# Eight experts finished before the next one's products, the last tile's shift on TensorE and its rows stored in halves, and one weight load moved

## The chip, the core and the metric

The kernel runs on one core of a Trainium2 chip, in one launch. The metric is the device time of that launch in microseconds (us), the median of several runs. The engines are named as in the profile: PE is TensorE (PEld its weight loads), DVE VectorE, ACT ScalarE, POOL GpSimd, SP SyncE. SyncE only issues DMAs here; ScalarE and GpSimd issue some too.

## What is computed

One layer of a diffusion trunk, on 128 context tokens and 512 latent tokens of width 1024. A modulation from a condition vector, a mixing sub-layer (windowed attention beside a gated MLP over chunks, then an output projection) and a channel sub-layer, a mixture of 32 experts, of which each token takes two:

```
h2 = rms_norm(x, g_pre_ffn) * (1 + scale2) + shift2
g_prob = softmax(h2 @ router_group); g_top, g_idx = top_k(g_prob, 1)
e_top, e_idx = top_k(expert logits of that group, 2)
weights = softmax(e_top) * g_top
hid = silu(h2 @ w_gate[e]) * (h2 @ w_up[e])          # per chosen expert
f = sum over the two experts of weight * (hid @ w_down[e])
x = x + gate2 * rms_norm(f, g_post_ffn)
```

Each expert has w_gate, w_up (1024 x 256) and w_down (256 x 1024) in float32: 1 MB each, 3 MB for an expert, 96 MB in all.

## The kernel before, in words

The 640 tokens are five tiles of 128 (TILES = 5; the last is number 4, `KEPT`). The program is written out engine by engine, with semaphores between them; there is no scheduler, and each engine runs its instructions in the order in which its block writes them.

In the tail of the mixing sub-layer, for each tile, TensorE does the output projection (L762), VectorE the residual, and three things follow from it. TensorE turns the residual (`turn_res`) and makes the router's logits (`router`), from which VectorE makes the choice of experts (`route`, L1311 to L1334) and each token's rank in its expert (`rank`); TensorE helps with `prefix` and `pick`. GpSimd multiplies the residual by the scale (L1787), ScalarE by the token's norm (`scaled`, L1652), GpSimd adds the shift (L1793, `st_bc[:, 1]`): this is h2, and a DMA stores it as rows in DRAM (`h2_dram`, in the profile `h_rows`). For tiles 0 to 3 SyncE issues the store, for the last one ScalarE (L1657). `keep_warm` issues matmuls whose result nobody reads.

When all rows are stored and the row indices are made (`rows_made`, L1373), GpSimd gathers for each expert the rows of its tokens by indirect DMAs (`gather`, L1800), up to 64 tokens in one tile; experts with more tokens have a second tile (`xg_x`, inside the `If` of each engine's `expert`). An expert is: turn the gathered rows (`next_x`), the gate and up products (`products`, L909), silu on ScalarE (L1682) and the multiplication on VectorE (L1440), turn the result (L532), the down product (L917), a copy, and a scatter of the result rows by GpSimd (L1809).

Two orders of this exist. With `late` false, expert e+1's gate and up products stand on TensorE ahead of expert e's down product. With `late` true, expert e's down product and its second tile come first, then `expert_done` is raised, and then follow expert e+1's products. `late = e < EARLY or e >= LATE`, with EARLY = 3 and LATE = 26.

The weights have seven slots (WS = 7), four in `ring`, the others in space that attention or the residual used (`w_5`, `w_5d`, `w_6`, `w_6d`, `w_7`; in the profile `w`, `w_5d`, `w_6d`). SyncE issues the loads in one queue. Expert e's load (from 7 on) waits for the down product and `expert_done` of expert e-7 and for the landing of expert e-2's (L454 and L455). The loads of experts 0 to 6 stand before that, between the stores of rows; the w_down of expert 4 (`load_down(4)`) is issued when the last tile's `mixg` is there.

Of the kernel before, what the change touches and what calls it, by code (L numbers as in the profile page):

```python
# [14 lines left out]
P = 128  # L15
# [3 lines left out]
TILES = (CTX + LAT) // P  # L19
# [27 lines left out]
XS = 3  # L47
LS = 4
LATE = EXPERTS - 6
EARLY = 3  # L50
KEPT = TILES - 1
ADDED = 3
GATE_SLOT = 25
# [58 lines left out]
def hybrid_dit_step(  # L112
# [4 lines left out]
    with ExitStack() as ctx:  # L117
# [74 lines left out]
        rows = sb("rows", [N_ROWS, P], F32, b0 + 2 * KB)  # L192
        gm_u = sb("gm_u", [P, TILES, GM], F32, b0)
        h2 = sb("h2", [P, 2, D], F32, b0)
# [20 lines left out]
        st_bc = sb("st_bc", [P, 2, D], F32, t0 + 4 * KB)  # L215
# [50 lines left out]
        def const(name):  # L266
            a, b = CONST_COLS[name]
            return cst[:, a:b] if b <= N_KEPT else cst_once[:, a - N_KEPT:b - N_KEPT]

        ident = const("ident")  # L270

        ps = ctx.enter_context(nc.psum_tensor("ps", [P, 8, 512], F32))
# [3 lines left out]
        h2_dram = nc.dram_tensor("h2_rows", [TILES * P, D], F32, kind="Internal").ap()  # L276
# [31 lines left out]
        op0_mm, op_mm, sq2, ms2, rs2, mixg, res1, sq3, ms3, rs3 = (  # L308
            sem(n) for n in ("op0_mm", "op_mm", "sq2", "ms2", "rs2", "mixg", "res1", "sq3", "ms3", "rs3"))
        t2_tr, t2_dve, t2_act, h2_mul, h2_sc, h2_done = (  # L310
            sem(n) for n in ("t2_tr", "t2_dve", "t2_act", "h2_mul", "h2_sc", "h2_done"))
        h2_out = [sem("h2_out0"), sem("h2_out1")]
        st_in, w_made, sh_mm = (sem(n) for n in ("scale_shift_in", "router_made", "shift_mm"))
# [65 lines left out]
        def _(sp):  # L379
# [64 lines left out]
            def load_down(e):  # L444
                sp.dma_start(weights(e)[1], w_down[0, e].rearrange("(k p) f -> p k f", p=P)).then_inc(wd_in[e % LS], 16)
# [44 lines left out]
            load_half(5, 1)  # L490
            sp.wait_ge(op_mm, TILES)
            load_expert(RING - 1)
            sp.wait_ge(mixg, 2 * TILES)
            load_down(4)
            sp.wait_ge(rt_mm, TILES)
            sp.wait_ge(sq3, 2 * TILES)
            sp.wait_ge(h2_out[0], 16 * 3)
            sp.wait_ge(h2_out[1], 16 * 2)
            for j in range(XS):
                sp.wait_ge(xg_in[j], 16)  # L500
            sp.wait_ge(rows_made, ALL_ROWS)
            sp.wait_ge(w_made, W_TOK)
            sp.wait_ge(e_in, 16)
# [26 lines left out]
        def _(pe):  # L530
# [99 lines left out]
            for i in range(TILES):  # L630
                if i >= 2:
                    pe.wait_ge(kv_read, i - 1)
                for k in range(KC):
                    last = pe.matmul(ps[:, i % 2, 0:2 * KVW], h_t[:, k, i * P:(i + 1) * P], w_kv[:, k, :],
                                     start=(k == 0), stop=(k == KC - 1))
# [56 lines left out]
            for i in range(TILES):  # L692
# [3 lines left out]
                for cc in range(4):  # L696
                    last = transpose(ps[:, 4 + i % 4, cc * P:(cc + 1) * P], gm_u[:, i, cc * P:(cc + 1) * P])
# [140 lines left out]
            def prefix(i):  # L838

                pe.wait_ge(r_both, i + 1)  # L840
                if i:
                    pe.wait_ge(r_rank, i)
                for m in range(i + 1):
                    last = pe.matmul(ps[:, 7, 64:64 + EXPERTS], before_b[:, :] if m == i else ones_b[:, :], both[:, m, :],
                                     start=(m == 0), stop=(m == i))
                last.then_inc(r_pos, 1)
# [24 lines left out]
            def keep_warm(n):  # L871

                for _ in range(n):
                    pe.matmul(ps[:, 2, :], ident, mix_t[:, KEPT, 0:4, :].rearrange("p k q -> p (k q)"), start=True, stop=True)

            prefix(TILES - 2)
            pe.wait_ge(mixg, 2 * (TILES - 1))
            pe.wait_ge(sq2, 2 * (TILES - 1))
            keep_warm(3)
            turn_res(TILES - 1)  # L880
            router(TILES - 1)
            pick(TILES - 2)
            keep_warm(3)
            prefix(TILES - 1)
            pick(TILES - 1)
            pe.wait_ge(r_rank, TILES)
            for m in range(TILES):
                last = pe.matmul(ps[:, 7, 96:96 + EXPERTS], ones_b[:, :], both[:, m, :], start=(m == 0), stop=(m == TILES - 1))
            last.then_inc(r_idx, 1)
            keep_warm(2)  # L890

            def pick_extras():
# [43 lines left out]
            def expert(e):  # L936
                c = e
                wgu, wd = weights(e)
                late = e < EARLY or e >= LATE
                xb = e % 2 if late else (e + 1) % 2  # L940
# [42 lines left out]
        def _(dve):  # L983
# [458 lines left out]
            def expert(e):  # L1442
                c = e
                late = e < EARLY or e >= LATE
                xb = e % 2 if late else (e + 1) % 2
# [52 lines left out]
        def _(act):  # L1498
# [41 lines left out]
            for z, ks in enumerate(((1,), (3,), (6, 7))):  # L1540
                act.wait_ge(s_pre, z + 1)
                for k in ks:
                    for cn, (a, b) in enumerate(((0, P), (P, TILES * P))):
                        last = act.activation(h_t[:, k, a:b], h_t[:, k, a:b], ACT.Identity,
                                              bias=pre[:, 0, 1, k, cn:cn + 1], scale=pre[:, 0, 0, k, cn:cn + 1])
# [21 lines left out]
            for u in range(2 * TILES):  # L1567
                i = u % TILES
# [78 lines left out]
            def scaled(i):  # L1647
                act.wait_ge(rs3, i + 1)
                for hh in range(2):
                    act.wait_ge(h2_mul, 2 * i + hh + 1)  # L1650
                    part_ = h2[:, i % 2, 512 * hh:512 * (hh + 1)]
                    act.activation(part_, part_, ACT.Copy, scale=stats[:, 7, i:i + 1]).then_inc(h2_sc, 1)  # L1652
                if i < KEPT:
                    act.dma_start(out_rows(i), res[:, i]).then_inc(res_out, 16)
                else:
                    act.wait_ge(h2_done, 2 * TILES)
                    act.dma_start(h2_dram[i * P:(i + 1) * P, :], h2[:, i % 2]).then_inc(h2_out[i % 2], 16)  # L1657

            act.wait_ge(w_made, 1)
            for i in range(TILES):  # L1660
# [23 lines left out]
            def expert(e):  # L1684
                c = e
                late = e < EARLY or e >= LATE
                if not late:
# [42 lines left out]
        def _(pool):  # L1730
# [31 lines left out]
            for t in range(TILES * PAIRS):  # L1762
                i = t // PAIRS
                w = P * (1 if i == 0 else 3 if i in (1, 4) else 4)
                pool.wait_ge(inv_made, t + 1)
                for a in range(KVH):
                    p = probs[:, t % 4, a, 0:w]
                    last = pool.tensor_scalar(p, p, att_stats[:, INV, t, a:a + 1], 1.0, ALU.mult, ALU.mult)  # L1768
# [8 lines left out]
            for i in range(TILES):  # L1777
                pool.wait_ge(ms2, i + 1)
                rsqrt(stats[:, 4, i:i + 1], stats[:, 3, i:i + 1], 1, rs2)
                if i < 2:  # L1780
                    pool.wait_ge(st_in, 16 * (i + 1))
                else:
                    pool.wait_ge(h2_out[i % 2], 16 * (i // 2))
                for hh in range(2):
                    pool.wait_ge(res1, 2 * i + hh + 1)
                    cut_ = slice(512 * hh, 512 * (hh + 1))
                    pool.tensor_tensor(h2[:, i % 2, cut_], res[:, i, cut_], st_bc[:, 0, cut_], ALU.mult).then_inc(h2_mul, 1)  # L1787
                pool.wait_ge(ms3, i + 1)
                rsqrt(stats[:, 7, i:i + 1], stats[:, 6, i:i + 1], 1, rs3)
                for hh in range(2):  # L1790
                    pool.wait_ge(h2_sc, 2 * i + hh + 1)
                    cut_ = slice(512 * hh, 512 * (hh + 1))
                    pool.tensor_tensor(h2[:, i % 2, cut_], h2[:, i % 2, cut_], st_bc[:, 1, cut_], ALU.add).then_inc(h2_done, 1)  # L1793
# [38 lines left out]
                                            y_x[:, :], None, bounds_check=2 * TOPK * TILES * P - 1,  # L1832
                                            oob_is_err=False).then_inc(e_st, 16)

            pool.wait_ge(h2_out[0], 16 * 3)
            pool.wait_ge(h2_out[1], 16 * 2)
            pool.wait_ge(rows_made, FIRST_ROWS)
            for c in range(XS):
# [15 lines left out]
            for e in range(EXPERTS):  # L1854
                late = e < EARLY or e >= LATE
                if not late:
# [46 lines left out]
```

## Time and profile before

| what | before |
|---|---|
| median of 3 runs | 634.27 us (633.21 to 635.83) |
| the profiled execution | 633.7 us, its span 631.8 us |
| TensorE busy | 541.1 us, 86% of the span |
| VectorE, ScalarE, GpSimd busy | 183.5, 149.5, 178.1 us |
| read and written in DRAM | 163.75 and 16.68 MB, 286 GB/s over the span |
| expert stage, from the first gather | 333.9 us to the end |
| the chain that ended last, by engine | TensorE 66%, DMA 23%, VectorE 4%, the rest 7% |
| granted TensorE clock, mean | 0.956 |

Busy time is the time in which an engine had an instruction running; a high share does not say that the engine bounds the kernel. Which wait ends last in a stage is read from the chain and from the waits. A clock of 1.00 in the windows is 2.4 GHz, 0.50 is 1.2 GHz. A DMA share of 1.00 in a window means that all 16 DMA engines worked all the time.

### The profile page before, as it was taken

The numbers are of one execution on the slowest core, as the hardware profiler recorded it, in microseconds if no ns is written. First come the engines' busy times: TensorE is split into PE (matmuls) and PEld (weight loads), VectorE is DVE, ScalarE is ACT, GpSimd is POOL, SyncE is SP. The second block draws the span as 40 slices with busy tenths as digits, with TensorE's granted clock in tenths as the row PEclk, the third lists the DMA queues.
The fourth block names the chain that finished last, engine by engine and source line by source line (L and its number), as shares of the span: only waits on it lengthen the run. The fifth ranks groups of instructions, "written<-read, shape, count | busy, mean of one in ns | idle before, by whom it ended". The sixth has DMA issues, their size and how long they took to land.

```text
span 631.8 us, 10117 instructions
## 1 busy us (share of the span) xinstructions
PE 541.1 (86%) x3527; PEld 309.2 (49%) x3527; DVE 183.5 (29%) x581; ACT 149.5 (24%) x374; POOL 178.1 (28%) x247
## 2 busy tenths in 40 slices
PE   2899999999889999999977799899998888878700
PEld 2654764444666664555534455565655444434300
DVE  2210340002368861444485111111111101111026
ACT  4401021012047761222230111111111111111133
POOL 1000300014404440344445233243433123321214
PEclk9999999999998999999996999999999888999965
DMA  9999742060799304421692999799999999999178
GB/s 321 369 380 387 225 171 98 16 251 0 206 303 408 154 1 170 170 93 68 240 383 72 399 409 396 275 409 405 406 401 399 381 397 402 398 410 408 70 311 203
DMA packets 59075, 173.21 MB, mean 274 GB/s; under 512 B 5804, under 2 KB 11492, under 8 KB 58112
## 3 DMA queue, kind: packets, MB, share of 16 engines
q1 hardware_dynamic: 50608, 153.76, 64.5%
q0 software_dynamic: 7216, 15.77, 8.0%
q10 hardware_dynamic: 1184, 2.81, 1.2%
q8 instruction: 40, 0.66, 0.4%
q14 instruction: 27, 0.22, 0.1%
HBM read 163.75 MB, written 16.68 MB: 286 GB/s over the span
## 4 chain that ended last, share of the span: by engine, by line
PE 66%; DMA 23%; DVE 4%; issue 2%; ACT 2%; SPq 1%; POOL 1%; ACTq 0%; POOLq 0%; DVEq 0%
PE ps L909 12%; PE ps L762 11%; PE ps L652 11%; PE ps L532 8%; DMA ring<-in_w_down_dram 8%; PE ps L917 6%; PE ps L606 6%; DMA ring<-in_w_up_dram 4%; PE ps L549 4%; DMA w<-in_w_down_dram 3%; PE ps L714 3%; DMA w_6d<-in_w_down_dram 3%; PE ps L739 2%; DMA out_dram<-v_all 1%; DMA cst_once<-in_consts_dram 1%
## 5 line engine op out<-in xcount | busy, mean ns | idle before, releaser
L909 PE MATMUL ps<-ring,xt 128*64 128x256 f32 x704 | 84.9, 396 | 14.9 <-DMA ring<-in_w_up_dram 10.6
L909 PEld LDWEIGHTS ps<-ring,xt 128*64 128x64 f32 x704 | 55.3, 142 | 51.0 <-DMA ring<-in_w_up_dram 16.8
L652 PE MATMUL ps<-ring,h_t 128*128 128x512 f32 x160 | 69.5, 593 | 0.0
L1440 DVE TENSOR_TENSOR hid<-act_g,ps 128x128 f32<-128x128 f32 x32 | 9.2, 288 | 198.0 <-ACT act_g L1682 198.0
L909 PE MATMUL ps<-w,xt 128*64 128x256 f32 x416 | 49.4, 391 | 8.1 <-DMA w<-in_w_up_dram 5.2
L762 PE MATMUL ps<-ring,mix_t 128*128 128x512 f32 x120 | 53.6, 596 | 0.0
L1809 POOL DMA_INDIRECT expert_results<-y_sb,idx_out x32 | 32.5, 1015 | 63.6 <-ACT y_sb L1696 62.2
L652 PEld LDWEIGHTS ps<-ring,h_t 128*128 128x128 f32 x160 | 30.1, 190 | 36.8 <-issue 36.8
L909 PEld LDWEIGHTS ps<-w,xt 128*64 128x64 f32 x416 | 33.5, 140 | 27.8 <-DMA w<-in_w_up_dram 8.8
L1800 POOL DMA_INDIRECT xg<-h_rows,idx_in x32 | 34.6, 1081 | 28.2 <-POOL idx_in L1798 22.5
L917 PE MATMUL ps<-ring,hid_t 128*64 128x512 f32 x160 | 38.7, 605 | 2.5 <-ACT hid_t L1692 2.5
L1682 ACT ACTIVATE act_g<-ps 128x128 f32<-128x128 f32 x32 | 8.9, 277 | 133.5 <-PE ps L909 133.5
L606 PE MATMUL ps<-ring,h_t 128*128 128x512 f32 x80 | 35.6, 597 | 1.9 <-issue 1.9
L762 PEld LDWEIGHTS ps<-ring,mix_t 128*128 128x128 f32 x120 | 22.2, 190 | 25.8 <-issue 25.7
L1768 POOL TENSOR_SCALAR probs<-probs,att_stats 128x384 f32<-128x384 f32 (+2 forms) x40 | 22.9, 586 | 42.1 <-DVE att_stats L1220 42.1
L1733 POOL TENSOR_TENSOR stats<-stats,half_pow 128x1 f32<-128x1 f32 x20 | 15.4, 772 | 67.7 <-DVE stats L1264 40.5
L1696 ACT COPY y_sb<-ps 128x512 f32<-128x512 f32 x32 | 18.7, 585 | 66.5 <-PE ps L917 66.5
L1733 POOL TENSOR_TENSOR gm_stats<-gm_stats,half_pow 128x8 f32<-128x8 f32 x5 | 9.7, 1942 | 80.4 <-DVE gm_stats L1161 80.4
L549 PE MATMUL ps<-ring,cond 128*32 128x128 f32 x768 | 24.5, 281 | 1.6 <-issue 1.5
L1798 POOL COPY idx_in<-src_row 128x1 uint32<-128x1 uint32 x29 | 5.3, 184 | 71.6 <-PE ps L532 71.6
L549 PEld LDWEIGHTS ps<-ring,cond 128*32 128x32 f32 x768 | 21.4, 113 | 6.5 <-issue 6.1
L606 PEld LDWEIGHTS ps<-ring,h_t 128*128 128x128 f32 x80 | 14.7, 190 | 19.5 <-issue 19.5
(243 smaller groups left out, 732.1 us busy)
## 6 DMA issues: line engine op xcount, KB each, us to landing
ring<-in_w_mod_dram SPq DMA_DIRECT2D x10, 2048.0 KB, 12.4
ring<-in_w_gate_dram SPq DMA_DIRECT2D x20, 1024.0 KB, 9.4
ring<-in_w_up_dram SPq DMA_DIRECT2D x20, 1024.0 KB, 14.4
ring<-in_w_down_dram SPq DMA_DIRECT2D x20, 1024.0 KB, 16.5
w<-in_w_gate_dram SPq DMA_DIRECT2D x12, 1024.0 KB, 8.0
w<-in_w_up_dram SPq DMA_DIRECT2D x12, 1024.0 KB, 13.5
y_back<-expert_results SPq DMA_DIRECT2D x5, 1024.0 KB, 8.8
ring<-in_w_mod_dram SPq DMA_DIRECT2D x4, 1024.0 KB, 12.8
```

What stands on the lines that cost most here:

```text
L532: return pe.matmul(out, in_, ident[0:n_in, 0:n_in], is_transpose=True, start=True, stop=True)
L549: last = pe.matmul(ps[32 * g:32 * g + 32, b % 2, 0:P], cond[:, k, :], w[:, k, g * P:(g + 1) * P], start=(k == 0), stop=(k == KC - 1))
L606: last = pe.matmul(ps[:, 3 + i, 0:ATT], h_t[:, k, i * P:(i + 1) * P], w_q[:, k, :], start=(k == 0), stop=(k == KC - 1))
L652: last = pe.matmul(ps[:, 4 + u % 4, :], h_t[:, k, i * P:(i + 1) * P], w[:, k, :], start=(k == 0), stop=(k == KC - 1))
L714: last = pe.matmul(ps[:, 2 * (t % 2) + a, pos * P:(pos + cnt) * P], q_t[half, g, i * P:(i + 1) * P], k_t[half, first * P:(first + cnt) * P ...
L762: last = pe.matmul(ps[:, 2 * (i % 2) + hh, :], mix_t[:, i, k, :], rhs, start=(k == 0), stop=(k == KC - 1))
L909: last = pe.matmul(bank[fh * SLOT:(fh + 1) * SLOT, 0:FE].rearrange("p (a f) -> p a f", a=2), x_t[:, k % 4, (k // 4) * SLOT:(k // 4 + 1) * ...
L917: last = pe.matmul(bank[ch * SLOT:(ch + 1) * SLOT, :], h[:, fh * SLOT:(fh + 1) * SLOT], w[:, fh, ch * 512:(ch + 1) * 512], start=(fh == 0) ...
L1733: pool.tensor_tensor(dst, src, half_pow[:, 0:n], ALU.pow).then_inc(done, 1)
L1768: last = pool.tensor_scalar(p, p, att_stats[:, INV, t, a:a + 1], 1.0, ALU.mult, ALU.mult)
L1800: pool.indirect_dma_start(xg[:, j, :], None, h2_halves, bass.IndirectOffsetOnAxis(ap=idx_in[:, j, 0:1], axis=0), bounds_check=2 * TILES * ...
L1809: pool.indirect_dma_start(y_halves, bass.IndirectOffsetOnAxis(ap=idx_out[:, c, 0:1], axis=0), y_buf(e), None, bounds_check=2 * TOPK * TILE ...
```

## The change

`EARLY` goes from 3 to 8, so experts 3 to 7 change to the `late` order on all engines. For the last tile, TensorE adds the shift: it first writes the shift into two PSUM banks by an identity matmul, then accumulates the scaled h2 on top, half by half; ScalarE copies each half back into `h2` and issues its store. GpSimd leaves out its addition for that tile. Two groups of three `keep_warm` matmuls go, and the last group of two waits for ScalarE's copies, as it writes the same bank. In SyncE's queue `load_down(4)` moves behind the waits for the stored rows and for the first three gathers. The counts on `h2_out[0]` rise by one store.

```diff
-EARLY = 3
+EARLY = 8
@@ SyncE
-            sp.wait_ge(mixg, 2 * TILES)
-            load_down(4)
             sp.wait_ge(rt_mm, TILES)
             sp.wait_ge(sq3, 2 * TILES)
-            sp.wait_ge(h2_out[0], 16 * 3)
+            sp.wait_ge(h2_out[0], 16 * 4)
             sp.wait_ge(h2_out[1], 16 * 2)
             for j in range(XS):
                 sp.wait_ge(xg_in[j], 16)
+            sp.wait_ge(mixg, 2 * TILES)
+            load_down(4)
@@ TensorE
+            def last_shift(rows):
+                for hh in range(2):
+                    cut_ = slice(512 * hh, 512 * (hh + 1))
+                    if rows:
+                        pe.wait_ge(h2_sc, 2 * KEPT + hh + 1)
+                    last = pe.matmul(ps[:, 2 + hh, :], ident, h2[:, KEPT % 2, cut_] if rows else st_bc[:, 1, cut_],
+                                     start=not rows, stop=rows)
+                    if rows:
+                        last.then_inc(sh_mm, 1)
...
-            keep_warm(3)
+            pe.wait_ge(st_in, 16 * 2)
+            last_shift(False)
             turn_res(TILES - 1)
             router(TILES - 1)
             pick(TILES - 2)
-            keep_warm(3)
+            last_shift(True)
...
+            pe.wait_ge(h2_done, 2 * TILES)
             keep_warm(2)
@@ ScalarE
-                    act.wait_ge(h2_done, 2 * TILES)
-                    act.dma_start(h2_dram[i * P:(i + 1) * P, :], h2[:, i % 2]).then_inc(h2_out[i % 2], 16)
+                    for hh in range(2):
+                        half = slice(512 * hh, 512 * (hh + 1))
+                        act.wait_ge(sh_mm, 3 + hh)
+                        act.copy(h2[:, i % 2, half], ps[:, 2 + hh, :]).then_inc(h2_done, 1)
+                        act.wait_ge(h2_done, 2 * i + hh + 1)
+                        act.dma_start(h2_dram[i * P:(i + 1) * P, half], h2[:, i % 2, half]).then_inc(h2_out[i % 2], 16)
@@ GpSimd
-                for hh in range(2):
+                for hh in range(2 if i < KEPT else 0):
                     pool.wait_ge(h2_sc, 2 * i + hh + 1)
...
-            pool.wait_ge(h2_out[0], 16 * 3)
+            pool.wait_ge(h2_out[0], 16 * 4)
```

How the instructions stand on TensorE around the last tile, as a difference (`res` is the residual, `h_92` is h2, `cst` the identity):

```order
 L844 MATMUL ps<-both,before_b 128x32
-L874 MATMUL ps<-mix_t,cst 128x512 x3
+L881 MATMUL ps<-st_bc,cst 128x512 x2
 L532 MATMUL ps<-cst,res 128x128 x8
 L834 MATMUL ps<-w_rs,res_t 128x36 x8
 L852 MATMUL ps<-code_oh,sel_slot 128x64 x2
-L874 MATMUL ps<-mix_t,cst 128x512 x3
+L881 MATMUL ps<-h_92,cst 128x512 x2
 L844 MATMUL ps<-both,ones_b 128x32 x4
 L844 MATMUL ps<-both,before_b 128x32
```

Both groups of three are gone; in their places stand the shift (from `st_bc`) and the scaled rows.

TensorE from expert 3's products on, before (`w_129` holds expert 4's gate and up weights, `hid` is expert 3's):

```order
L909 MATMUL ps<-ring,xt 64x256 x16
L532 MATMUL ps<-cst,xg 128x128 x4
L909 MATMUL ps<-w_129,xt 64x256 x16
L532 MATMUL ps<-cst,hid 128x128
L532 MATMUL ps<-cst,xg 128x128 x4
L917 MATMUL ps<-ring,hid_t 64x512 x4
```

The same place after the change (lines after `last_shift` are 12 higher, so L909 is L921 and L917 is L929):

```order
L921 MATMUL ps<-ring,xt 64x256 x16
L532 MATMUL ps<-cst,xg 128x128 x4
L532 MATMUL ps<-cst,hid 128x128
L929 MATMUL ps<-ring,hid_t 64x512 x4
...
L966 UNCONDITIONAL_BRANCH
L921 MATMUL ps<-w_129,xt 64x256 x16
L532 MATMUL ps<-cst,xg 128x128 x4
```

Expert 4's products have moved behind expert 3's down product and the branch around its second tile.

SyncE's queue around `load_down(4)` (`w_5d`), as a difference, with the semaphores that each waits for:

```order
 L440 DMA ring<-in_w_up_dram 128x2x1024
 L445 DMA ring<-in_w_down_dram 128x2x1024
-L445 DMA w_5d<-in_w_down_dram 128x2x1024 [waits mixg]
-L445 DMA w_6d<-in_w_down_dram 128x2x1024 [waits xg_in1,xg_in2,xg_in0,rows_made,h2_out1,router_made,h2_out0,extra_in,sq3,rt_mm]
+L445 DMA w_5d<-in_w_down_dram 128x2x1024 [waits xg_in0,xg_in1,h2_out1,xg_in2,h2_out0,mixg,sq3,rt_mm]
+L445 DMA w_6d<-in_w_down_dram 128x2x1024 [waits extra_in,router_made,rows_made]
 L440 DMA w_133<-in_w_gate_dram 128x2x1024
```

The waits for the stored rows and the gathers now stand ahead of the load of `w_5d` and no longer behind it.

## Rows read from the trace of the kernel before

**Rows 1.** Pieces of the chain that ended last in order of time: start us, us, what
```profile
474.26 17.14 DMA w<-in_w_down_dram
...
575.51 3.67 PE ps L909 x32
```

**Rows 2.** Waits of SyncE's DMA queue, 300 to 600 us: total us, times, longest us
```profile
SPq L455 <- PEq L965: 48.2, 7, 14.0
SPq L454 <- DMA ring<-in_w_up_dram: 47.3, 13, 4.9
...
SPq L503 <- DMA xg_x<-h_rows,idx_x: 3.4, 1, 3.4
```

**Rows 3.** Timeline, SyncE's queue: start us, us, engine line op out<-in
```profile
345.96 0.37 SPq L445 DMA_DIRECT2D w_6d<-in_w_down_dram  x1
...
364.62 0.37 SPq L440 DMA_DIRECT2D ring<-in_w_gate_dram  x1
...
371.53 0.37 SPq L440 DMA_DIRECT2D ring<-in_w_gate_dram  x1
...
383.07 0.37 SPq L440 DMA_DIRECT2D ring<-in_w_gate_dram  x1
...
398.82 0.37 SPq L440 DMA_DIRECT2D w<-in_w_gate_dram  x1
...
405.28 0.37 SPq L440 DMA_DIRECT2D w<-in_w_gate_dram  x1
...
411.45 0.37 SPq L440 DMA_DIRECT2D w<-in_w_gate_dram  x1
...
419.30 0.37 SPq L440 DMA_DIRECT2D ring<-in_w_gate_dram  x1
```

**Rows 4.** Windows: from:to us, length, busy us of five engines, PEclk, DMA share, GB/s
```profile
332.00:346.00 14.00, 11.09 (x64) 6.38 (x66) 8.39 (x35) 0.54 (x2) 8.93 (x11) 0.67 0.24 67
347.00:395.00 48.00, 41.83 (x301) 24.53 (x297) 6.80 (x14) 6.75 (x18) 15.72 (x25) 1.00 1.01 398
394.00:401.00 7.00, 4.71 (x33) 2.31 (x31) 0.29 (x1) 1.13 (x3) 1.32 (x3) 1.00 0.34 95
401.00:575.00 174.00, 155.92 (x1073) 87.19 (x1069) 23.50 (x48) 27.26 (x74) 56.45 (x93) 0.97 1.02 401
```

**Rows 5.** The chain again: expert 4's second tile is turned
```profile
389.27 0.69 PE ps L532 x4
```

**Rows 6.** Timeline, tile 3 and the last tile: start us, us, engine line op
```profile
299.74 0.23 DVE L1319 TENSOR_SCALAR r_e<-r 128x4 f32<-128x4 f32 x1
...
322.58 0.58 ACT L1645 COPY res_t<-ps 128x512 f32<-128x512 f32 x1
...
325.15 2.82 PE L874 MATMUL ps<-mix_t,cst 128*128 128x512 f32 x6
...
325.52 1.33 ACT L1652 ACTIVATE h<-h,stats 128x512 f32<-128x512 f32 x2 [1.74 <-POOL stats L1733]
...
326.32 2.48 POOL L1793 TENSOR_TENSOR h<-h,st_bc 128x512 f32<-128x512 f32 x2 [0.83 <-ACT h L1652]
...
326.67 0.94 DVE L1319 TENSOR_SCALAR r_e<-r 128x4 f32<-128x4 f32 x1
...
327.53 1.30 DVE L1320 TENSOR_SCALAR r_e<-cst,r_s 128x4 f32<-128x4 f32 x1
...
332.43 0.22 DVE L1373 TENSOR_SCALAR idx_in<-ps,cst 128x3 uint32<-128x3 f32 x1 [0.38 <-PE ps L852]
...
333.89 1.17 POOL L1800 DMA_INDIRECT xg<-h_rows,idx_in  x1 [5.08 <-DMA h_rows<-h]
```

**Rows 7.** The chain again: the store of the last tile's rows
```profile
328.83 4.19 DMA h_rows<-h
```

**Rows 8.** DMAs that touch h_rows, 240 to 345 us
```profile
DMA to landing us min/median/max: 2.6/2.9/5.6
```

**Rows 9.** Windows, the microsecond in which the granted clock falls
```profile
331.00:332.00 1.00, 0.08 (x4) 0.00 (x0) 0.85 (x4) 0.62 (x1) 0.00 (x0) 0.53 0.96 393
```

## The prediction

> **What bounds the kernel now.** I read the page's chain first. Its shares (in the table above) name TensorE for two thirds and DMA for a quarter, which is an average over stages. So I read the chain in order of time next. It runs through TensorE until 474 us; from there to 575.5 it holds only weight loads and their issues, the first of them 17.14 us from issue to landing [rows 1]; then come the last two experts on TensorE and the end. The weight stream alone sets the time at which the last expert can be computed. A faster TensorE in the stream's own stretch is worth nothing; what counts is when the stream gets started and whether it ever stands still.
>
> The waits of SyncE's queue say when it does. It waited for TensorE's "expert done" seven times, 48.2 us in total, and after that for landings [rows 2]. Those seven are the loads of experts 7 to 13, since expert e's load takes the slot of expert e-7. Issued were expert 5's w_down at 345.96, expert 8 at 364.62, 9 at 371.53, 10 at 383.07, 11 at 398.82, 12 at 405.28, 13 at 411.45 and 14 at 419.30 [rows 3]. I then looked at what the 16 DMA engines did at these times. From 347 to 395 they were full, share 1.01. Before, from 332 to 346, they had a share of 0.24. And from 394 to 401 there is a hole: seven microseconds at a share of 0.34, so 7 x 0.66 = 4.6 us in which the DMA engines had nothing, because expert 11's load was not issued before 398.82. From 401 to 575 the share is 1.02 [rows 4]. So there are two holes, one of 4.6 us behind expert 4 and one ahead of 347, and the change touches both.
>
> **Eight experts in the late order.** Experts 3 to 7 now do transpose, down product, second tile and "done" before the next expert's gate and up products. This adds no instruction. In the late order an expert without a second tile takes 371.53 - 364.62 = 6.91 us from slot to slot [rows 3]. Expert 2 is done at 371.53 as before. Expert 3 then is done at 378.44 instead of 383.07. Expert 4 would be done at 385.35 without its second tile, which ran from 389.27 [rows 5] to the issue at 398.82 and costs 9.55; it ends at 394.90. Expert 11's load is issued 3.9 us earlier from this part alone. The loads of 12 and 13 follow at 6.91 each, which is less than the roughly 10 us that the full stream took for an expert at that point ((419.30 - 398.82)/2, as expert 14 waits for expert 12's landing), so no new hole opens.
>
> The late order also costs TensorE something, since the handoffs through ScalarE and VectorE are bare: 6.91 us against the 411.45 - 405.28 = 6.17 of an expert in the other order [rows 3], so some 0.7 for each of five experts, 3.7 us in all. The stream hides it: it needs some 10 us for an expert, so TensorE has slack from expert 8 on. Without that cover it is a loss, which is a rival below. GpSimd's gather three experts ahead now stands behind the scatter and the second tile; it still has more than two experts, over 13 us, so I price it at nothing.
>
> **The last tile's shift on TensorE.** GpSimd's two additions, 2.48 us from 326.32, go [rows 6]. In their place come two 512-wide matmuls that lay down the shift early, beside the wait for the residual (nothing), two with h2, and two copies on ScalarE. A kept-warm matmul of the same shape took 2.82/3 = 0.94, a 512-wide copy from PSUM 0.58 [rows 6]. The scaled halves are ready at about 326.2 and 326.85 (325.52 + 1.33). The matmuls end at about 327.2 and 328.1, the second copy at 328.7, and the second half is issued at about 328.8. Before, the whole store was issued at 328.83 [rows 7]. So the addition itself is worth nothing on that path; only the first half leaves 0.9 earlier.
>
> What it does give is on VectorE. Two tiny operations of the last route took 0.94 and 1.30 while GpSimd was adding, and ended with its two halves; the same line took 0.23 for tile 3 with GpSimd quiet [rows 6]. Without the additions 2.24 - 0.46 = 1.8 us leave the path to the row indices: they stand at 332.65 - 1.8 = 330.85 instead of 332.65. This is bounded below by nothing, if something else holds VectorE, and above by the 1.8.
>
> **Store in halves and the moved load.** The store of the last tile took 4.19 us [rows 7] with the DMA engines full; the usual one of these rows took 2.9 [rows 8]. The change takes 1 MB (expert 4's w_down) out of that queue: 1.05 MB at 400 GB/s is 2.6 us. It halves what the last store carries. For the second half I have no row: 1.45 us if it were proportional to bytes, 4.19 if nothing helps. I take 2.5, near the quiet store of 2.9. It lands at 331.3, after the indices; the gathers began 0.87 after the landing before (333.02 to 333.89) [rows 6, 7], so now at about 332.2, that is 1.7 us earlier. The ends are 2.2 (indices decide, 330.85 + 0.87) and 0.
>
> The Trainium skill (DMA: Bandwidth & Descriptors, section Anatomy of one DMA) speaks against halves: each DMA pays a fixed part of about 2.0 us whatever its size, mostly the confirmation of the last byte. By it, the half would take an estimated 2.0 + 0.26 MB at 436 GB/s = 2.6 us and the gathers would start 1.6 earlier, not 2.2. The trace agrees so far that its 512 KB stores never took less than 2.6 [rows 8].
>
> Everything on TensorE from the gathers to expert 4 follows them, so it moves by these 1.7. The moved load is issued when the three first gathers have landed. SyncE waited for the extra gather 3.4 us up to 345.96 [rows 2, 3], so they had landed by 342.5, now by 340.8; the load fills the hole ahead of 347 and is needed only at expert 4. Queued behind it are the wait for the extra gather and the loads of 5 and 6. That gather now shares the engines with 1 MB, which may cost it between 0 and 2.6 us. I take 0.9, so the stream begins 0.8 earlier rather than 1.7.
>
> **Sum.** Expert 11's load is issued 3.9 + 1.7 = 5.6 us earlier. The stream in front of it ends 0.8 earlier, so there are 4.6 + 0.8 = 5.4 us of hole that can be closed, and the hole closes wholly. The gain is the smaller, 5.4 us, and the stream hands it on to the end, since it is full from 401 to the last load and what follows is unchanged. The profiled execution took 633.7 (span 631.8 and 1.9 around it) and would take 628.3. It lay 0.6 below the median of 634.27; against the median I predict 628.9.
>
> **Rivals.** (1) The gathers don't start earlier: the half store lands late, or the matmuls are slow. Speaking for it: the clock. The granted clock fell to 0.53, near the lower of its two levels (1.2 against 2.4 GHz), after TensorE had stood still from 328.0 [rows 6, 9]; the change takes out warming matmuls and has TensorE wait twice for other engines in this tile. At half clock the two h2 matmuls take 1.9 each, the store leaves about 1.9 later and eats the 1.7. Against it: it still did its work at full clock after shorter stops. The gain is then 3.9, 630.4. The Trainium skill (TensorE: Matmul & The Clock Gate, Part 1) has the slow clock as the default that recent activity lifts; by it this rival is open, and no run here shows yet where TensorE's fall would now come.
>
> (2) The hole stays for the larger part, as the weights' order or the gather of the extra rows, not TensorE's slot, sets expert 11's issue. Speaking for it: the extra gather of the second tile is issued by GpSimd, whose order changed. Against it: it is in flight since the tile before. Half of 3.9 remains, 632.3.
>
> (3) Slower: the end is set by TensorE, not by the stream. Its place is experts 3 to 13, its price the five bare handoffs, 3.7 us, less the 1.7 from the gathers: 2.0 slower, 636.3; with rival 1 it is 3.7 slower, 638.0. It decides if TensorE still waits for no weights after 474. The chain's TensorE pieces up to 474 speak for it, SyncE's landing waits from expert 14 on and the full DMA share against it.
>
> **How the numbers follow.** Forecast 0.62, rival 1 0.20, rival 2 0.12, rival 3 0.06. A change of 0.5%, 3.2 us, is about what can be told from none, so faster means below 631.1. Nearly all of the forecast and three quarters of rival 1 lie there, 0.77; within are what is left of both and rival 2 but for a hundredth, 0.16; slower are rival 3 and that hundredth, 0.07. The likeliest case alone spans 628.2 (the gathers 2.2 earlier and the hole no limit: 3.9 + 2.2 = 6.1) to 629.6 (the gathers 0.8 earlier: 4.7). The range takes in rival 1 whole and rival 2 up to its value and leaves 1.2 us below the likeliest case, about the 1.1 by which the lowest of the three runs lies under their median: 627.0 to 632.3.
>
> **What would show it.** Right: expert 11's load issued near 393, DMA share near 1 from 346 to the last load, the issues from expert 14 on about 5.4 earlier; the two tiny VectorE operations at 0.23; the gathers near 332.2; expert 4's w_down near 341. Wrong: a hole in the DMA share elsewhere between 346 and 401; a granted clock of 0.5 before 328; the last store landing after 332; or TensorE instead of loads in the chain behind 474.

## The result and the profile after

| | before | changed |
|---|---|---|
| median of 20 runs | 634.22 us | 631.38 us |
| ratio, 95% interval | | 0.9949 (0.9933 to 0.9965) |
| profiled execution, its span | 633.7, 631.8 us | 628.56, 626.7 us |

One of the 20 runs of each kernel took over 1900 us; the medians count it, while the ratios, here and below, leave out runs over 1.5% above the fastest of their kernel (also 683.11 us in move_only, and 636.17 in warm3_all_late, with which its ratio would be some 0.001 higher). By the ratio the change gives 3.2 us, 2.1 to 4.3; the medians differ by 2.8. The two profiled executions differ by 5.1, but 1.76 of that was there before the first changed instruction. The load of expert 3, which no edit touches, was issued at 318.84 before and at 317.08 after. From here on I count times in the last tile and behind it from that issue, and call it L3. The last row of results is made by VectorE at L3 + 307.17 before (626.01) and at L3 + 303.59 after (620.67), a gain of 3.6 within the changed stretch. (A second trace of the changed kernel, in the table below, has 1.7.)

SyncE's queue after the change; the first row is L3, the others are the loads of expert 5's w_down and of experts 8 to 12, 14 and 15 (start us, us, engine line):

```profile
317.08 0.37 SPq L440 DMA_DIRECT2D ring<-in_w_gate_dram  x1
...
344.70 0.37 SPq L445 DMA_DIRECT2D w_6d<-in_w_down_dram  x1
...
362.72 0.37 SPq L440 DMA_DIRECT2D ring<-in_w_gate_dram  x1
...
369.77 0.37 SPq L440 DMA_DIRECT2D ring<-in_w_gate_dram  x1
...
377.81 0.37 SPq L440 DMA_DIRECT2D ring<-in_w_gate_dram  x1
...
393.47 0.37 SPq L440 DMA_DIRECT2D w<-in_w_gate_dram  x1
...
400.64 0.37 SPq L440 DMA_DIRECT2D w<-in_w_gate_dram  x1
...
414.63 0.37 SPq L440 DMA_DIRECT2D ring<-in_w_gate_dram  x1
...
426.19 0.37 SPq L440 DMA_DIRECT2D ring<-in_w_gate_dram  x1
```

Against [rows 3]: expert 8's load is at L3 + 45.64 (before 45.78) and expert 9's at 52.69 (52.69), so nothing came early before the reordered experts. Expert 11's is at L3 + 76.39 (79.98), 3.6 earlier. Expert 5's w_down is at L3 + 27.62 (27.12), half a microsecond later. The windows, to be laid beside [rows 4] (from:to us, busy us of five engines, granted clock, DMA share, GB/s):

```profile
319.00:321.00 2.00, 0.87 (x6) 0.63 (x7) 1.73 (x3) 0.90 (x3) 0.79 (x1) 1.00 1.01 408
321.00:323.00 2.00, 1.89 (x15) 1.69 (x13) 1.52 (x2) 1.02 (x3) 2.00 (x2) 0.82 1.04 426
323.00:329.00 6.00, 5.45 (x18) 2.92 (x18) 3.77 (x24) 2.51 (x4) 0.64 (x2) 0.50 0.70 278
392.00:399.00 7.00, 5.39 (x41) 3.54 (x41) 0.98 (x2) 1.13 (x3) 1.39 (x4) 1.00 0.80 290
399.00:573.00 174.00, 159.75 (x1116) 91.17 (x1114) 23.48 (x48) 27.37 (x73) 58.73 (x96) 0.98 1.02 402
```

The hole behind expert 4 has gone from 4.6 to 7 x 0.20 = 1.4 us, and behind it the stream is full, as before. The other thing to see is the clock in the first three rows. It falls to 0.50 (1.2 GHz) in the last tile; before, it stayed at 1.00 there until 331. Two rows of the kernel before, the router's matmuls and the window ahead of its fall [rows 9]:

```profile
323.31 1.95 PE L834 MATMUL ps<-w_rs,res_t 128*128 128x36 f32 x16
...
330.00:331.00 1.00, 0.21 (x5) 0.19 (x5) 0.90 (x6) 0.98 (x3) 0.00 (x0) 1.00 1.06 422
```

The last tile after the change in the timeline, against [rows 6]:

```profile
321.55 2.92 PE L834 MATMUL ps<-w_rs,res_t 128*128 128x36 f32 x16
...
324.54 3.78 PE L881 MATMUL ps<-h,cst 128*128 128x512 f32 x4
...
325.59 0.23 DVE L1331 TENSOR_SCALAR r_e<-r 128x4 f32<-128x4 f32 x1
325.73 0.22 DVE L1332 TENSOR_SCALAR r_e<-cst,r_s 128x4 f32<-128x4 f32 x1
...
328.36 0.59 ACT L1671 COPY h<-ps 128x512 f32<-128x512 f32 x1 [1.12 <-PE ps L881]
...
328.97 0.33 ACTq L1673 DMA_DIRECT2D h_rows<-h  x1
...
329.75 0.22 DVE L1385 TENSOR_SCALAR idx_in<-ps,cst 128x3 uint32<-128x3 f32 x1 [0.33 <-PE ps L852]
...
331.88 1.48 POOL L1816 DMA_INDIRECT xg<-h_rows,idx_in  x1 [8.15 <-DMA h_rows<-h]
```

VectorE's two small operations are at 0.23 and 0.22, as forecast. The two h2 matmuls took 3.78 instead of the 1.88 forecast. The second half left at L3 + 11.89, 1.9 later than the whole store before (9.99). The chain says what its landing took (answers to [rows 7]):

```profile
328.97 2.04 DMA h_rows<-h
```

That is 2.04 instead of 4.19. So it landed 0.2 us earlier than before, and the gathers started at L3 + 14.80 against 15.05.

### The profile page after: what moved, and what is told of

Same layout as the page of the kernel before. It is cut to its first block, busy times and chain, and to the rows that moved or that the text cites. A ratio compares the mean times of both kernels' runs of the same rounds, so it can differ in the third digit from the quotient of the medians.

```text
span 626.7 us, 10110 instructions
## 1 busy us (share of the span) xinstructions
PE 538.8 (86%) x3523; PEld 308.4 (49%) x3523; DVE 181.7 (29%) x581; ACT 150.8 (24%) x376; POOL 175.2 (28%) x245
## 4 chain that ended last, share of the span: by engine, by line
PE 60%; DMA 29%; DVE 3%; issue 2%; SPq 2%; ACT 2%; POOL 1%; ACTq 0%; POOLq 0%; DVEq 0%
PE ps L762 11%; PE ps L652 11%; DMA ring<-in_w_down_dram 11%; PE ps L921 8%; PE ps L532 7%; PE ps L606 6%; PE ps L929 4%; DMA ring<-in_w_up_dram 4%; PE ps L549 4%; DMA w_5d<-in_w_down_dram 4%; PE ps L714 3%; DMA w<-in_w_down_dram 3%; DMA w_6d<-in_w_down_dram 3%; PE ps L739 2%; DMA ring<-in_w_mod_dram 2%
## 5 line engine op out<-in xcount | busy, mean ns | idle before, releaser
L921 PE MATMUL ps<-ring,xt 128*64 128x256 f32 x704 | 83.1, 389 | 12.4 <-DMA ring<-in_w_up_dram 7.1
L921 PEld LDWEIGHTS ps<-ring,xt 128*64 128x64 f32 x704 | 55.4, 140 | 46.1 <-issue 13.6
L921 PE MATMUL ps<-w,xt 128*64 128x256 f32 x416 | 49.4, 391 | 5.0 <-DMA w<-in_w_up_dram 2.7
L921 PEld LDWEIGHTS ps<-w,xt 128*64 128x64 f32 x416 | 33.8, 140 | 25.1 <-issue 10.4
L929 PE MATMUL ps<-ring,hid_t 128*64 128x512 f32 x160 | 38.7, 605 | 3.3 <-ACT hid_t L1708 2.8
L532 PE MATMUL ps<-cst,xg 128*128 128x128 f32 x128 | 22.5, 302 | 4.3 <-DMA xg<-h_rows,idx_in 4.3
L1613 ACT ACTIVATE probs<-probs,att_stats 128x384 f32<-128x384 f32 (+2 forms) x40 | 24.0, 600 | 0.0
```

The costliest lines, as they stand in the source:

```text
L532: return pe.matmul(out, in_, ident[0:n_in, 0:n_in], is_transpose=True, start=True, stop=True)
L921: last = pe.matmul(bank[fh * SLOT:(fh + 1) * SLOT, 0:FE].rearrange("p (a f) -> p a f", a=2), x_t[:, k % 4, (k // 4) * SLOT:(k // 4 + 1) * ...
L929: last = pe.matmul(bank[ch * SLOT:(ch + 1) * SLOT, :], h[:, fh * SLOT:(fh + 1) * SLOT], w[:, fh, ch * 512:(ch + 1) * 512], start=(fh == 0) ...
L1613: last = act.activation(probs[:, t % 4, a, 0:width(t)], probs[:, t % 4, a, 0:width(t)], ACT.Exp, bias=att_stats[:, NM, t, a:a + 1], scale= ...
```

## The experiments

All ratios are to the kernel before, run on the same chip at the same time (the interval is of 95%). Since the edits are worth 1 or 2 us, the better instrument is the trace, counted from L3. The table gives TensorE's clock in the h2 matmuls, the issue of the (second half) store, the first gather, the load of expert 5's w_down, expert 11's load, and the last result row.

| kernel | ratio | clock | store | gather | w_down 5 | load 11 | last row |
|---|---|---|---|---|---|---|---|
| before | 1 | - | 9.99 | 15.05 | 27.12 | 79.98 | 307.17 |
| changed | 0.9949 | 0.5 | 11.89 | 14.80 | 27.62 | 76.39 | 303.59 |
| changed, again | 0.9942 (0.9923-0.9961) | 0.5 | 11.77 | 14.67 | 29.77 | 77.41 | 305.49 |
| early_only | 0.9966 (0.9940-0.9992) | - | 10.00 | 15.03 | 26.97 | 77.25 | 305.42 |
| tail_only | 1.0001 (0.9977-1.0026) | 0.5 | 11.89 | 14.78 | 27.90 | 79.79 | 306.70 |
| move_only | 0.9971 (0.9952-0.9989) | - | 9.99 | 14.78 | 27.45 | 79.99 | 307.42 |
| early5 | 0.9995 (0.9974-1.0016) | 0.5 | 11.89 | 14.80 | 27.04 | 76.35 | 306.83 |
| warm | 0.9935 (0.9909-0.9961) | 1.0, then 0.5 | 11.46 | 14.37 | 27.01 | 75.85 | 304.01 |
| warm2 | 0.9916 (0.9883-0.9948) | 1.0 | 10.23 | 13.13 | 26.48 | 74.74 | 303.03 |
| warm3 | 0.9927 (0.9900-0.9955) | 1.0 | 10.23 | 13.12 | 27.22 | 74.58 | 302.41 |
| warm3, again | 0.9929 (0.9904-0.9954) | 1.0 | 10.22 | 13.13 | 26.77 | 75.86 | 303.86 |
| warm3_nomove | 0.9928 (0.9904-0.9951) | 1.0 | 10.23 | 15.06 | 26.91 | 76.41 | 304.32 |
| warm3_all_late | 0.9919 (0.9886-0.9952) | 1.0 | 10.23 | 13.13 | 27.36 | 76.43 | 304.56 |
| extra_first | 0.9915 (0.9889-0.9940) | 1.0 | 10.23 | 13.13 | 26.03 | 73.44 | 301.37 |

The two kernels that were profiled twice show what one trace is worth. Up to the first gather they agree within 0.15 us; expert 11's load moves by 1.0 and 1.3 and the last row by 1.9 and 1.5, among other things because expert 0's products run at the lower clock for a varying part (they took 4.25 us in the changed kernel's first trace and 5.43 in its second) and because the gather of the second tile landed 3.3 us after its issue in the one and 5.6 in the other. In two rows the second trace missed what was expected of it below: the clock fell at L3 + 7.4, not within 6, and expert 11's load came at 77.41, not at 76.2 to 76.5.

**One part at a time.** The late order alone (early_only), the rest alone (tail_only), the moved load alone (move_only):

```diff
-EARLY = 3        # early_only: the kernel before with
+EARLY = 8
-EARLY = 8        # tail_only: the changed kernel with
+EARLY = 3
```

> The kernel before with EARLY = 8 and nothing else. Theory A (the late order of experts 3 and 4 is all that the change gained; the rest came to nothing because TensorE's clock fell in the last tile): expert 11's load comes about 3.7 us earlier after the load of expert 3 than before (76.3 instead of 80.0 us), the hole in the DMA share behind expert 4 shrinks from 4.6 to about 1 us, and the time is about 3.5 us below before, like the whole change. Rival B (the moved load and the last tile gave part of it): less than 2.5 us below before.

> The changed kernel with EARLY back at 3: the last tile's shift on TensorE, the halved store and the moved load alone. Theory A: the granted clock falls to half in the router's matmuls of the last tile, the gathers start as long after the load of expert 3 as before (14.8 to 15.1 us), and the time is that of before within 1 us. Rival B: 1.5 us or more below before.

The last tile's edits and the moved load without the late order give nothing, as theory A said, and the hole stays. The late order alone gives 2.2 us by the ratio (0.5 to 3.8), short of the 3.5 expected and inside what rival B allowed, though the interval takes in both and the medians differ by 3.1. Its expert 11's load came 2.7 earlier and not 3.7; in this trace expert 0's products took 5.30 us instead of 4.37, at the lower clock for the first three and a half. The hole behind expert 4 shrinks to 7 x 0.20 = 1.4 us, as in the changed kernel. The windows of tail_only and of early_only:

```profile
392.30:399.30 7.00, 4.70 (x33) 2.30 (x31) 0.29 (x1) 1.13 (x3) 1.33 (x3) 1.00 0.41 140
390.00:397.00 7.00, 5.77 (x42) 3.35 (x43) 0.00 (x0) 0.81 (x2) 1.20 (x2) 1.00 0.80 283
```

I can't tell its 2.2 from the whole change's 3.2: the intervals overlap.

> The kernel before with only the load of expert 4's w_down moved. Theory A: the last tile's store takes about 3 us instead of 4.2, the gathers start about 0.4 us earlier at most, since the row indices then decide (332.65 in the kernel before), the hole behind expert 4 stays, and the time is that of before within 0.5 us. Rival B: over 1 us faster.

```diff
             sp.wait_ge(op_mm, TILES)
             load_expert(RING - 1)
-            sp.wait_ge(mixg, 2 * TILES)
-            load_down(4)
...
                 sp.wait_ge(xg_in[j], 16)
+            sp.wait_ge(mixg, 2 * TILES)
+            load_down(4)
```

The whole store took 2.6 us instead of 4.2, with the load out of its way. Gathers 0.3 earlier and then nothing, as expected: the indices, ready at L3 + 13.81 in the kernel before, now decide. Expert 11's load is where it was before, and the last row within 0.3. The ratio nonetheless says 1.8 us faster (0.7 to 3.0). No row of the trace has that, and I leave it open; it is a warning against reading the ratios of the other kernels to the microsecond.

**Only experts 3 and 4 in the late order.**

```diff
-EARLY = 8
+EARLY = 5
```

> The changed kernel with EARLY = 5, so only experts 3 and 4 change their order. Theory A (the hole is behind expert 4, so only these two matter): the time of the changed kernel within 0.7 us. Rival E (the loads of experts 12 to 14 also have to come early): a new hole in the DMA share after expert 11's load, and 1 us or more slower than the changed kernel.

Theory A fell, rival E was right. Windows of early5, in which L3 is 318.15:

```profile
393.00:400.00 7.00, 4.93 (x40) 3.40 (x40) 0.98 (x2) 0.86 (x2) 1.38 (x3) 1.00 0.77 262
400.00:404.00 4.00, 4.00 (x37) 3.01 (x34) 0.16 (x1) 0.47 (x2) 1.05 (x1) 1.00 1.02 415
404.00:408.00 4.00, 4.00 (x29) 2.15 (x30) 0.82 (x2) 0.64 (x2) 1.80 (x4) 1.00 0.36 96
```

Expert 11's load comes as early as with EARLY = 8, but the DMA engines stand again 4 x 0.64 = 2.6 us in the third row. The loads of experts 11 and 12 show why:

```profile
394.50 0.37 SPq L440 DMA_DIRECT2D w<-in_w_gate_dram  x1
406.14 0.37 SPq L440 DMA_DIRECT2D w<-in_w_gate_dram  x1
```

They lie 11.6 apart. Expert 4, the last late one, is followed by the products of 5, and expert 5, back in the other order, has those of 6 ahead of its own down product. So the products of two experts lie between two releases of a slot. With EARLY = 8 that pause lies between the loads of experts 14 and 15 (414.63 to 426.19 above, also 11.6), where the loads of experts 13 and 14 are still under way and the DMA engines stay full (share 1.02 or 1.03 from 414 to 430). The late order has to reach as far as the stream has no reserve, not only to the expert with the hole.

**The clock.** Is the missing gain the clock? First one warmer ahead of the shift matmuls, as many microseconds of work as the three warmers before:

```diff
+            keep_warm(1)
             last_shift(False)
```

> The changed kernel with one warming matmul (0.94 us) ahead of the two that lay down the shift, so that TensorE has the same 2.8 us of work there as before. Theory A: the granted clock stays at 1.0 until the h2 matmuls are done, these take 1.9 us instead of 3.8, the second half store leaves 1.5 to 1.9 us earlier relative to the load of expert 3, the gathers start 1.5 us or more earlier, and the time is 1.5 us below the changed kernel, some 5 us below before. Rival C (the clock falls anyway, as TensorE stands before the h2 matmuls): half clock at the h2 matmuls as in the changed kernel, and its time. Rival D (the clock stays, but the gathers' landings, not their start, hold the experts): gathers earlier, no time gained.

Rival C, mostly. Windows of warm (L3 is 317.50):

```profile
321.50:323.50 2.00, 1.90 (x18) 1.69 (x17) 1.60 (x2) 0.95 (x3) 2.00 (x2) 1.00 1.03 422
323.50:325.50 2.00, 1.01 (x7) 0.65 (x7) 1.13 (x9) 1.31 (x2) 0.56 (x2) 0.98 1.03 422
325.50:327.50 2.00, 2.00 (x4) 0.65 (x2) 1.73 (x12) 0.61 (x2) 0.00 (x0) 0.50 0.67 262
```

The clock holds through the router's matmuls, but TensorE then stands about 1 of 2 us waiting for ScalarE (second row), and beside the h2 matmuls the clock is at 0.50 (third row; they take 3.35). In the four traces of kernels with the changed kernel's tile it fell between L3 + 5.1 and 7.4, here at 7.9. So that stop was filled too, with a matmul into bank 4, whose turned residual has been copied out by then, and a third one stands behind the h2 matmuls (`keep_warm` takes the bank as a second argument here):

```diff
             pick(TILES - 2)
+            keep_warm(1, 4)
             last_shift(True)
+            keep_warm(1, 4)
             prefix(TILES - 1)
```

> The changed kernel with three warming matmuls: one ahead of the shift, one between the pick of tile 3 and the h2 matmuls, one behind them (the last two into a PSUM bank that is free by then). With one warmer the granted clock fell 7.9 us after the load of expert 3, while TensorE stood 1 us before the h2 matmuls. Theory A: with that stop filled the clock stays at 1.0 there, the second half store is issued at about 10.0 us after the load of expert 3 instead of 11.9, the gathers start at about 13.0 instead of 14.8, and expert 11's load comes some 1.7 us earlier than in the changed kernel; the time is 1.5 us below it. Rival C: the clock falls all the same and nothing is gained over the kernel with one warmer. Rival F: the store leaves earlier but the row indices or the descriptors hold the gathers at 14 or later.

Windows of warm2 (L3 is 316.93), the same three stretches as shown for the changed kernel, and its timeline:

```profile
319.00:321.00 2.00, 1.72 (x9) 0.79 (x8) 1.58 (x3) 1.05 (x3) 0.94 (x1) 1.00 0.99 383
321.00:323.00 2.00, 1.90 (x18) 1.69 (x16) 1.62 (x2) 0.87 (x3) 1.93 (x2) 1.00 1.02 420
323.00:329.00 6.00, 4.92 (x27) 2.23 (x26) 4.42 (x26) 3.96 (x7) 0.55 (x1) 1.00 0.83 326
```

```profile
324.39 1.98 PE L881 MATMUL ps<-h,cst 128*128 128x512 f32 x4
...
327.16 0.33 ACTq L1676 DMA_DIRECT2D h_rows<-h  x1
...
328.68 0.22 DVE L1388 TENSOR_SCALAR idx_in<-ps,cst 128x3 uint32<-128x3 f32 x1 [0.33 <-PE ps L852]
...
330.06 1.17 POOL L1819 DMA_INDIRECT xg<-h_rows,idx_in  x1 [6.48 <-DVE dst_row L1388]
```

The clock stays at 1.00, the matmuls take 1.98, the store leaves 1.7 earlier than in the changed kernel, and the gathers start at L3 + 13.13, 1.9 before the old 15.05. Expert 11's load is 5.2 earlier than before. Theory A held in every row that it named. The ratio is 5.3 us below before (3.3 to 7.4).

With more warmers at the end, until the first rows land:

```diff
-            keep_warm(2)
+            keep_warm(5)
```

> The same with five warming matmuls instead of two behind the last pick, so that TensorE works until the first gathered rows land. Theory A: the turning of the first rows and expert 0's products run at full clock, 1.3 instead of 1.95 us and 3.7 instead of 4.3, so expert 11's load comes up to 1.2 us earlier than in the kernel with three warmers. Rival: the clock was full again by then anyway, or falls in the wait of the gathers whatever is done, and the time is the same within 0.3 us.

The first rows are turned in 1.41 (1.92 in warm2) and expert 0's products take 3.67 (4.65), so the clock is held there as well. But TensorE then only waits for the gathered rows of expert 0's second tile, which became the late one. Expert 11's load gains 0.2, not 1.2 (and in the second trace of warm3 it comes 1.1 later than warm2's).

> warm3 once more, on the same chip as the changed kernel: if the clock is what the change lost, 1.0 to 1.8 us below the changed kernel; if the forecast's term for the gathers is simply not there, the same within 0.5 us.

> The changed kernel once more, for comparison on one chip: 0.9949 of before, clock falling to 0.5 within 6 us after the load of expert 3, expert 11's load 76.2 to 76.5 us after it.

On one chip the medians are 630.18 and 630.85, the ratios 0.9929 and 0.9942: 0.8 us apart, with overlapping intervals, between the two cases that were expected. The last row is 1.6 earlier with the warmers, the difference of the two first traces was 1.2. The direction is the same in all comparisons of kernels that hold the clock (0.9915 to 0.9929) with the changed one (0.9942, 0.9949); the size in total time stays uncertain.

**The moved load, with the clock held.** warm3 with the load back at its place:

```diff
             load_expert(RING - 1)
+            sp.wait_ge(mixg, 2 * TILES)
+            load_down(4)
...
                 sp.wait_ge(xg_in[j], 16)
-            sp.wait_ge(mixg, 2 * TILES)
-            load_down(4)
```

> The same with the load of expert 4's w_down back at its old place, ahead of the last tile's store. Theory A (moving it was about neutral: it frees the queue for the store but then shares the engines with the gather of the second tile): the second half store takes 3 to 4 us instead of 2.0, the gathers start 0.5 to 1.5 us later, the loads of experts 5 and 6 are issued no later, and the time is 0 to 1 us above. Rival G (the moved load costs more than it gives, through the late gather of the second tile): the time is below that with the load moved.

The chain of warm3_nomove (L3 is 318.98), and of warm3 (L3 is 317.70), where the store and the gather of the second tile stand:

```profile
329.21 3.97 DMA h_rows<-h
```

```profile
327.93 2.03 DMA h_rows<-h
...
339.92 4.92 DMA xg_x<-h_rows,idx_x
```

Behind the old place of the load the half store takes 3.97, and the gathers start 1.9 later. Moved, it takes 2.03, and it is the gather of the second tile that shares the engines with it and takes 4.92; before, that one landed 2.9 after its issue, in warm3_nomove 2.8. Expert 11's load is 1.8 (or, by the second trace of warm3, 0.5) earlier with the load moved, while the ratios are the same (0.9928, 0.9927). Theory A as far as the trace goes; the time doesn't settle it.

**All experts in the late order, and the second tile's gather first.** Two edits of warm3:

```diff
-EARLY = 8
+EARLY = EXPERTS
```

> The same with EARLY = 32, so every expert is in the late order and there is no change of order at expert 8. Theory A (from expert 8 on the stream is the bound and the late order hides under it): the interval of 11.6 us between the loads of experts 14 and 15 goes, no hole comes, and the time is the same or up to 0.7 us less. Rival H (TensorE needs the early order to keep up, the slower case of the prediction): 22 bare handoffs of 0.7 us can't all hide and the time is 2 us or more above.

The pause of 11.6 between experts 14 and 15 is 8.5, and the time is the same: 0.9919 beside 0.9927. (Its one trace has expert 11's load 1.9 and 0.6 later than the two of warm3, which is what single traces scatter.) TensorE hides the 0.7 us of eighteen more experts, 8 to 25; the last six had the late order already. This is rival 3 of the prediction put to the test, and it is out.

```diff
-            gather_ahead(0)
+            pool.wait_ge(x_tr, 1)
             pool.memset(xg_x[:], 0.0).then_inc(xg_zero, 1)
...
             gather_extra(0)
+            gather_ahead(0)
             gather_ahead(1)
```

> The kernel with seven added... more exactly: the changed kernel with the warmers of warm3 and, on GpSimd, the gather of the second tile's rows ahead of the gathers for experts 3 and 4. In warm3 TensorE stood 1.5 us for that gather (27.18 us after the load of expert 3) and SyncE waited for it before the loads of experts 5 and 6. Theory A: it is issued 1.7 us earlier and lands 1.5 to 2.5 us earlier, the loads of 5 and 6 are issued near 25.2 instead of 27.2, expert 11's load 1 to 1.5 us earlier than in warm3 (near 73.3 instead of 74.6), and the end 1 to 1.5 us earlier against the load of expert 3. Rival I: the gathers for experts 3 and 4 come too late and stop TensorE, or the contention with the moved load only shifts, and nothing is gained.

The gather is issued 1.6 earlier, takes 5.3 us, and so lands 1.2 and 0.7 earlier than in the two traces of warm3, less than the 1.5 to 2.5 expected. TensorE waits 0.2 for it instead of 1.5 (1.0 in the second trace). Expert 11's load is at L3 + 73.44, and the last row at 301.37, 1.0 before warm3's and 5.8 before the kernel before. The median was 628.92 against 630.85 of the changed kernel on the same chip and 634.80 of the kernel before. It beats the kernel before clearly. Its one trace is also ahead of all others, but of warm3 by less than the 1.5 that two traces of one kernel differ; by ratio it is level with warm2. Its lead over the changed kernel is 1.7 us by the ratios (0.9915, 0.9942), whose intervals overlap.

## Why the prediction was right, and by how much it missed

The forecast was 628.9 in a range of 627.0 to 632.3 and "faster"; measured were 631.38 and 0.5% less than before. The gain is 3.2 us of the 5.4 forecast. By the prediction's own bar for faster, 631.1, the median lies just above and the ratio (0.9949 x 634.27 = 631.0) just below. The mechanism is the one named; one term was mis-sized, and the time stayed in the range because that was drawn to take in rivals 1 and 2.

Some signs agree by luck. The profiled execution took 628.56, and 628.3 was forecast for it; the gathers began at 331.88 and expert 11's load at 393.47, where 332.2 and 393 were named. All of these owe 1.76 us to the head start that the trace had at L3.

- *The time hangs on when the stream starts and where it stands still.* Shown. Kernels that leave the hole (tail_only, move_only) keep expert 11's load and the last row where they were, and early5, which moves the hole, keeps the time.
- *The late order gives 3.9.* Held as far as it could be seen: expert 3 was done at L3 + 59.7 (59.6 worked out), the second tile cost expert 4 9.56 us (9.55), and expert 11's load came 3.6 earlier (2.6 in the second trace). The 0.3 that lack are in the distance from expert 3 to expert 4, 7.1 instead of 6.91.
- *"No new hole opens" behind it.* True, but the reason given was not the whole one. I had not seen the pause of 11.6 us that the end of the late order brings; it is covered at expert 15 and wasn't at expert 12 (early5).
- *The gathers start 1.7 earlier.* This is the failed term: 0.25. Two of its parts were right. VectorE's 1.8 went, the half store took 2.04 where 2.5 was taken, and in warm2, where the clock holds, the gathers start 1.9 earlier. What failed is the price of 0.94 for a 512-wide matmul, taken from a stretch with warmers that the change itself removed. At the lower clock the two h2 matmuls took 3.78 instead of 1.88, and the store left the 1.9 later that rival 1 names. The router's 2.92 instead of 1.95 cost the store nothing: in the second trace the router took 1.95, and in both the h2 matmuls began at L3 + 7.46, when ScalarE's first half was there. The same matmuls also took half of what VectorE had saved. The tokens' ranks on TensorE (L844) stand behind them, and the indices came at L3 + 12.67 instead of 13.59, 0.9 earlier and not 1.8 (11.75 in warm2). That is rival 1, to which I had given 0.20 and a gain of 3.9. The measured gain, 3.2 by the ratio and 2.8 by the medians, lies between it and the 1.95 of rival 2, whose mechanism no run shows.
- *The stream begins 0.8 earlier.* It began 0.5 later (2.6 in the second trace), since the moved load delays the gather of the second tile: that took 2.8 or 2.9 us in the three kernels with the load at its old place and 3.1 to 5.6 in the others; 0.9 more had been taken. SyncE waited 5.7 us for it instead of 3.4 [rows 2]:

```profile
SPq L503 <- DMA xg_x<-h_rows,idx_x: 5.7, 1, 5.7
```

- *The hole closes wholly, 5.4.* 3.2 of its 4.6 us closed. With the clock held (warm2, and warm3 twice), expert 11's load comes 5.2, 5.4 and 4.1 earlier than before, the last row 4.1, 4.8 and 3.3.
- *TensorE's slack hides the late order's handoffs.* Shown by warm3_all_late.

## What to carry to other kernels

Where a stream of loads bounds the end, count what each edit does to its start and to its holes, and look for the next hole at the place where an order changes back. A matmul that nobody reads may be holding the clock for the ones behind it: before taking it out, look at how long TensorE will stand there, and price the new matmuls at both clocks. Compare traces from a common instruction ahead of the change; here 1.8 of the 5.1 us between two profiled executions were no effect of it.

## What was not expected of the hardware

- The granted clock fell to 0.50 in the last tile after short stops of TensorE. In the changed kernel TensorE stood from 319.0 to 320.1, worked again, and the clock fell at 322.3 (L3 + 5.2). In its second trace it fell only at L3 + 7.4, at the end of a second stop, 1.0 us ahead of the h2 matmuls. The first stop (changed kernel) and the second (its second trace):

```profile
320.12 1.32 PE L532 MATMUL ps<-cst,res 128*128 128x128 f32 x8 [1.15 <-DVE res L1285]
324.81 3.66 PE L881 MATMUL ps<-h,cst 128*128 128x512 f32 x4 [0.98 <-ACT h L1664]
```

  With the first stop filled it fell at L3 + 7.9 (warm); with both filled and a third warmer behind the h2 matmuls it did not fall there (warm2). Which of the two last kept it up isn't shown. The Trainium skill (TensorE: Matmul & The Clock Gate, Part 1) describes a clock that activity has to earn; by that rule taking out warmers costs the real matmuls behind them, and the trace agrees, with 2.92 for 1.95 and 3.78 for warm2's 1.98.
- Two operations on 4 columns cost VectorE 2.24 us while GpSimd added 512-wide halves and 0.45 without. The Trainium skill (SBUF — State Buffer, Who interferes with whom) calls the pair of ports that both share an exclusive lock, held for the whole instruction, against VectorE instructions in a mode that uses two ports, `tensor_scalar` among those that can; by that rule they wait for the end of each half, and the trace agrees: the second of them ended at 328.83 and GpSimd's additions at 328.80 [rows 6].
- A 256 KB store landed in 2.04 and 2.03 us in a queue with little in it and in 3.97 behind 1 MB of loads (warm3_nomove), while 512 KB had taken at least 2.6 [rows 8]. The prediction's estimate for it by the Trainium skill (DMA: Bandwidth & Descriptors, Anatomy of one DMA) was 2.6; the measurement decides. That section gives its fixed part of about 2.0 us for DMAs issued by GpSimd, and this one is ScalarE's.
